# Column sums for the l2 norms of a four-mixer transformer block: one float32 product replaced by two float32r products on split squares

## The chip, the cores and the metric

The kernel runs on one core of a Trainium2 chip. The metric is the device time of one launch, in microseconds (us). The trace is one profiled execution on that core. The engines are named as the profile names them: PE is TensorE (PEld its weight loads), DVE is VectorE, ACT is ScalarE, POOL is GpSimd, SP is SyncE. SBUF is the on-chip memory, PSUM the banks into which TensorE writes.

## The reference, cut to what matters

Two layers (`DEPTH = 2`) over 512 tokens of width 1024. Each mixes four branches; the first is a gated delta rule, and its queries and keys (4 heads of 128 each) are normalised by head:

```
def l2norm(x, eps=1e-6):
    xf = x.astype(jnp.float32)
    return xf * lax.rsqrt(jnp.sum(xf * xf, axis=-1, keepdims=True) + eps)

qkv = jax.nn.silu(causal_dwconv(gdn_qkv, conv_w))
qa, ka, va = jnp.split(qkv, [GDN_HEADS * GDN_DK, 2 * GDN_HEADS * GDN_DK], axis=-1)
qa = l2norm(to_heads(qa, GDN_HEADS)) * GDN_DK ** -0.5
ka = l2norm(to_heads(ka, GDN_HEADS))
...
oa = gated_delta_chunked(qa, ka, va, beta, g)
```

## The kernel before

Activations lie with features on the 128 partitions and tokens along the free axis, so a head of queries or keys is one tile of 128 x 512: `aQ[:, 0:4]` and `aK[:, 0:4]`. A sum over a head is then a sum over partitions, and TensorE makes it as a product with a matrix of ones, which leaves the sum in every row of a PSUM bank.

All large products are made from split operands. A float32 number is split into a float32r part (`_hi`) and a float32r remainder (`_lo`), and a product is three passes: hi x hi, lo x hi, hi x lo. The weights come in units of 256 rows x 512 columns: SyncE loads them into `stage`, GpSimd rounds them (L581, `ring_hi`) and subtracts (L583, `ring_lo`) into a ring of four units, and TensorE consumes one unit in 24 matmuls of 512 columns (L1722, `unit`). GpSimd may fill a ring slot when TensorE has done with the unit four earlier.

Every engine has its own program order, written out by hand; semaphores tie them. TensorE runs the jobs `aq`, `ak`, `aab` and `av` (the raw queries, keys, gate columns and values) and puts small products between the units of `av`, in `value_unit`:

- after unit 0: `l2_sums(0, 1, 2, 3)`, the four query tiles (L1827)
- after unit 1: `gates_by_token` (L1833, writes tile `ab`), `l2_sums(4, 5, 6, 7)` for the keys, and the product `gc` (L1849)
- halfway through unit 2: `gt` (L1867), which first waits until VectorE has copied `gc` out (L1323)

ScalarE's order there: for the queries, Silu and then Square into `q_sq` (L727, L733); for the keys Silu; and, once the first query sum is there, four rounds of Square of key tile i (L733, into the same four slots of `q_sq`, so it waits for query sum i), Ln and Exp of query sum i (L738, L740). Then four small operations for the gates (L760 to L764), then Ln and Exp of the key sums.

VectorE's order there: the convolutions of the eight tiles (L1291, L1293), `qk_normed` of the four queries (L1299), the gate numbers (L1307 to L1319), `qk_normed` of the four keys, and the copy L1323.

The sums and the small tiles use the four PSUM banks `mix0` to `mix3` in turn. `gc` is in `mix1`, which key sum 4 held: TensorE can write it when `qk_normed(4)` has freed the bank.

Of the kernel before, what the change touches and what calls it, by code (L numbers as in the profile page):

```python
# [19 lines left out]
ALU = mybir.AluOpType  # L20
ACT = mybir.ActivationFunctionType
AX_X = mybir.AxisListType.X

P = 128
# [258 lines left out]
def mixer_keys():  # L283
# [50 lines left out]
    "a_LTm0": 10, "a_LTm1": 10, "a_S0": 3, "a_ab": 1, "a_arg": 16, "a_attd": 4, "a_dec": 4, "a_decc": 8, "a_ed": 4,  # L334
    "a_g": 2, "a_kbe": 4, "a_ln": 8, "a_lt": 4, "a_lt0": 4, "a_ltc": 4, "a_ltq": 4, "a_nrm": 4, "a_ohi": 4,
    "a_olo": 4, "a_one": 2, "a_out": 4, "a_qd": 4, "a_rhi": 2, "a_rs": 8, "a_sc": 3, "a_silu": 12, "a_small": 2,
    "a_smallact": 4, "a_sq": 8, "a_tap": 24, "a_z": 4, "a_zero": 1, "an_rs": 4, "an_sq": 4, "b_exp": 36, "b_fc": 3,
    "b_fexp": 3, "b_max": 12, "b_nm": 12, "b_ohi": 5, "b_olo": 5, "b_rhi": 9, "b_rlo": 9, "b_rp": 9, "b_share": 2,
    "b_sum": 3, "b_zinv": 1, "b_zln": 1, "big_done0": 43, "big_done1": 43, "big_done2": 38, "big_done3": 38,
    "big_free0": 43, "big_free1": 43, "big_free2": 38, "big_free3": 38, "c_act": 40, "c_add": 8, "c_bias": 3,  # L340
# [14 lines left out]
def hybrid_kernel(nc, ins, out):  # L355
    ctx = ExitStack()
    with ctx:
# [111 lines left out]
        def sem(name):  # L469
            if name not in sems:  # L470
                sems[name] = ctx.enter_context(nc.semaphore(name))
            return sems[name]
# [3 lines left out]
        def upto(name, count):  # L476

            return sem(name), count + layer[0] * PER_LAYER.get(name, 0)
# [45 lines left out]
        def f32(ap):  # L524
            return ap.bitcast(F32)
# [61 lines left out]
        def scalar_layer(act, l):  # L587
# [141 lines left out]
            def qk_squares(i):  # L729
                if i >= 4:  # L730
                    mix_wait(act, ("l2", i - 4))
                act.wait_ge(*upto("a_silu", i + 1))
                A(q_sq[:, i % 4, :], (aQ, aK)[i // 4][:, i % 4, :], ACT.Square).then_inc(sem("a_sq"), 1)  # L733

            def qk_root(i):

# [381 lines left out]
        def vector_layer(dve, l):  # L1118
# [176 lines left out]
            def qk_normed(i):  # L1295
                dve.wait_ge(*upto("a_rs", i + 1))
                b, _ = MIX["l2", i]
                t = (aQ, aK)[i // 4][:, i % 4, :]
                mix_free(STT(t, t, DK ** -0.5 if i < 4 else 1.0, mxb[b][:, :], ALU.mult, ALU.mult), ("l2", i))  # L1299

            for i in range(8):
                conv(i)
            for i in range(4):
                qk_normed(i)
            ps = mix_wait(dve, "ab")
            abv = ps[:, 0:32].rearrange("p (b c) -> p b c", b=4)
# [377 lines left out]
        def tensor_layer(pe, l):  # L1684
# [86 lines left out]
            def done(ins_, key):  # L1771
                ins_.then_inc(sem(home(key)[1]), 1)
# [50 lines left out]
            def l2_sums(*tiles):  # L1823
                for i in tiles:
                    ps = tile_of(("l2", i))
                    pe.wait_ge(*upto("a_sq", i + 1))
                    done(MM(ps[:, :], f32(ones_r[:, 0:1]).to_broadcast((P, P)), q_sq[:, i % 4, :], start=True, stop=True), ("l2", i))  # L1827

            def gates_by_token():
                ps = tile_of("ab")  # L1830
# [564 lines left out]
```

## Time and profile before

| | us |
|---|---|
| median of 3 runs | 2326.91 |
| lowest and highest | 2325.54, 2327.57 |
| span of the profiled execution, first to last instruction | 2324.0 |
| TensorE busy | 2297.4 (99% of the span) |
| GpSimd, VectorE, ScalarE busy | 1282.2, 851.0, 751.4 |
| mean granted TensorE clock | 0.997 |

The profiled execution has no other time of its own than its span; the median is 2.9 us above it, which is what lies before the first and after the last instruction and the difference between executions.

A row of the timeline gives start, duration, engine, line, operation, output<-inputs, shapes and count; in square brackets stand the idle time of the engine before it and what ended that. Rows of one engine can overlap: TensorE's matmuls are pipelined, so the distance between starts, and not a duration, says how long each one holds the engine. A VectorE or GpSimd operation that was ready but could not run yet has the waiting time inside its duration.

### The profile page before, as it was taken

What the parts mean: (1) busy time and instruction counts of PE and PEld (TensorE: products, weight loads), DVE (VectorE), ACT (ScalarE), POOL (GpSimd) and SP (SyncE); (2) the same over time, 40 slices, a digit from 0 to 9 for tenths busy, and PEclk for the clock granted to TensorE, in tenths of its full rate; (3) what the DMA queues carried; (4) which work ended last, traced back from release to release, by engine and by line L of the source; (5) the groups of instructions that cost most, each with busy time, mean ns of one, the idle gap of its engine ahead of it and who ended that gap; (6) DMA issues with size and microseconds to landing.
All of it is one profiled execution on the core that took longest, in us unless ns stands there. A gap on an engine that the chain in (4) does not pass through costs nothing.

```text
span 2324.0 us, 31844 instructions
## 1 busy us (share of the span) xinstructions
PE 2297.4 (99%) x13054; PEld 1870.2 (80%) x13054; DVE 851.0 (37%) x1350; ACT 751.4 (32%) x1505; POOL 1282.2 (55%) x732
## 2 busy tenths in 40 slices
PE   8999999999999999999999999999999999999998
PEld 7788877877877888888887888778778778888887
DVE  4543225334445521123355430254243445112233
ACT  5633226213035321122355341451230544112121
POOL 5513654554554566677655136546555445666874
PEclk9999999999999999999999999999999999999999
DMA  4311331322221243322222113213222213333331
GB/s 151 91 38 47 95 87 46 118 82 86 75 89 52 92 124 92 100 94 97 82 79 85 36 54 93 73 60 115 84 88 84 74 60 101 108 100 94 97 100 64
DMA packets 105904, 196.72 MB, mean 85 GB/s; under 512 B 8480, under 2 KB 18848, under 8 KB 105504
## 3 DMA queue, kind: packets, MB, share of 16 engines
q1 hardware_dynamic: 104608, 188.40, 26.8%
q10 hardware_dynamic: 1152, 6.29, 0.8%
q8 instruction: 104, 1.70, 0.3%
q14 instruction: 40, 0.33, 0.0%
HBM read 192.57 MB, written 2.10 MB: 84 GB/s over the span
## 4 chain that ended last, share of the span: by engine, by line
PE 96%; ACT 2%; DVE 2%; issue 1%; DMA 0%; DVEq 0%; ACTq 0%
PE big L1722 71%; PE mix L1722 9%; PE mix L1867 5%; PE big L2074 1%; PE mix L2042 1%; PE mix L2144 1%; PE mix L2053 1%; PE mix L1827 1%; PE mix L2272 0%; PE mix L2225 0%; PE mix L1781 0%; ACT o_hi L618 0%; PE mix L2209 0%; PE mix L2195 0%; PE mix L1999 0%
## 5 line engine op out<-in xcount | busy, mean ns | idle before, releaser
L583 POOL TENSOR_TENSOR ring_lo<-stage,ring_hi 128x1024 fp32r<-128x1024 f32 (+3 forms) x364 | 912.4, 2507 | 30.4
L581 POOL TENSOR_SCALAR ring_hi<-stage 128x1024 fp32r<-128x1024 f32 (+3 forms) x364 | 371.3, 1020 | 987.9 <-PE big L1722 906.6
L1722 PE MATMUL big<-h_hi,ring_hi 128*128 128x512 f32 (+1 forms) x1888 | 720.6, 382 | 3.0 <-DVE h_lo L1173 1.8
L1722 PE MATMUL big<-h_hi,ring_lo 128*128 128x512 f32 (+1 forms) x1888 | 709.3, 376 | 0.0
L1722 PE MATMUL big<-h_lo,ring_hi 128*128 128x512 f32 (+1 forms) x1888 | 709.2, 376 | 0.0
L1722 PEld LDWEIGHTS big<-h_hi,ring_hi 128*128 128x128 f32 x1888 | 355.4, 188 | 75.1 <-issue 8.6
L1722 PEld LDWEIGHTS big<-h_lo,ring_hi 128*128 128x128 f32 x1888 | 355.4, 188 | 65.7
L1722 PEld LDWEIGHTS big<-h_hi,ring_lo 128*128 128x128 f32 x1888 | 355.7, 188 | 62.9 <-issue 1.4
L1663 DVE TENSOR_TENSOR h_lo<-scr,h_hi 128x1024 fp32r<-128x1024 f32 x64 | 84.7, 1323 | 248.5 <-ACT h_hi L1091 248.5
L1722 PE MATMUL big<-ring_hi,h_hi 128*128 128x512 f32 x448 | 174.2, 390 | 0.0
L1722 PE MATMUL big<-ring_lo,h_hi 128*128 128x512 f32 x448 | 174.1, 390 | 0.0
L1722 PE MATMUL big<-ring_hi,h_lo 128*128 128x512 f32 x448 | 173.7, 389 | 0.0
L1091 ACT ACTIVATE h_hi<-scr 128x1024 fp32r<-128x1024 f32 x64 | 68.5, 1070 | 262.2 <-PE big L1722 260.2
L1674 DVE SCALAR_TENSOR_TENSOR scr<-big,scr 128x512 f32<-128x512 f32 x64 | 44.3, 692 | 254.5 <-ACT scr L1100 254.3
L1722 PE MATMUL mix<-ring_hi,h_hi 128*128 128x512 f32 x320 | 125.0, 391 | 0.0
L1722 PE MATMUL mix<-ring_hi,h_lo 128*128 128x512 f32 x320 | 124.6, 389 | 0.0
L1722 PE MATMUL mix<-ring_lo,h_hi 128*128 128x512 f32 x320 | 124.5, 389 | 0.0
L1100 ACT ACTIVATE scr<-big 128x512 f32<-128x512 f32 x64 | 38.3, 598 | 262.1 <-PE big L1722 261.3
L1722 PEld LDWEIGHTS big<-ring_hi,h_hi 128*128 128x128 f32 x448 | 84.1, 188 | 18.4 <-issue 0.7
L1722 PEld LDWEIGHTS big<-ring_hi,h_lo 128*128 128x128 f32 x448 | 84.1, 188 | 17.7
L1722 PEld LDWEIGHTS big<-ring_lo,h_hi 128*128 128x128 f32 x448 | 83.8, 188 | 18.0 <-POOL ring_lo L583 1.0
L1722 PE MATMUL big<-o_hi,ring_hi 128*128 128x512 f32 x224 | 90.2, 403 | 1.0 <-ACT scr L676 0.9
(304 smaller groups left out, 2758.0 us busy)
## 6 DMA issues: line engine op xcount, KB each, us to landing
stage<-in_w_in SPq DMA_DIRECT2D x168, 512.0 KB, 3.5
stage<-in_w_mlp_in SPq DMA_DIRECT2D x64, 512.0 KB, 3.7
stage<-in_w_mlp_out SPq DMA_DIRECT2D x64, 512.0 KB, 3.6
stage<-in_w_o SPq DMA_DIRECT2D x16, 512.0 KB, 3.6
stage<-in_w_br_a SPq DMA_DIRECT2D x8, 512.0 KB, 3.6
stage<-in_w_br_c SPq DMA_DIRECT2D x8, 512.0 KB, 3.6
stage<-in_w_br_d SPq DMA_DIRECT2D x8, 512.0 KB, 3.6
stage<-in_w_br_b SPq DMA_DIRECT2D x8, 512.0 KB, 3.6
```

What stands on the lines that cost most here:

```text
L581: nc.gpsimd.tensor_scalar(rH[jw][0:pp, r, 0:kk, 0:job.n], w, 1.0, 0.0, ALU.mult, ALU.add).then_inc(sem("w_hi"), 1)
L583: nc.gpsimd.tensor_tensor(rL[jw][0:pp, r, 0:kk, 0:job.n], w, f32(rH[jw][0:pp, r, 0:kk, 0:job.n]), ALU.subtract).then_inc(sem("w_ready"), 1)
L1091: A(hH[:, q:q + 2, :], fT[:, 2 * u:2 * u + 2, :], ACT.Copy).then_inc(sem("f_hi"), 1)
L1100: A(fT[:, 4 * g + i, :], ps[:, :], ACT.Relu).then_inc(sem("f_relu"), 1)
L1663: TT(hL[:, q:q + 2, :], fT[:, 2 * u:2 * u + 2, :], f32(hH[:, q:q + 2, :]), ALU.subtract).then_inc(sem("f_lo"), 1)
L1674: big_free(STT(fT[:, k, :], ps[:, :], 0.0, fT[:, k, :], ALU.max, ALU.mult), (f"up{g}", i))
L1722: ins_ = MM(o_, a_, r_, start=s0, stop=s1)
L1827: done(MM(ps[:, :], f32(ones_r[:, 0:1]).to_broadcast((P, P)), q_sq[:, i % 4, :], start=True, stop=True), ("l2", i))
L1867: return MM(o_, a_, b_, start=True, stop=True)
L2042: i = MM(c_bank[u][:, at:at + w], hv(cK, h)[:, j * P:(j + 1) * P], hv(cQ, h)[:, j * P:], start=opens, stop=True, skip_group_check=True)
L2053: MM(c_bank[u][:, :], rot_r[:, 2 * P:3 * P], part[:, u, :], start=False, stop=True, skip_group_check=True)
L2074: r = MM(c_out[e * DH:e * DH + DH, j * P:], cV[:, j, (2 * p + e) * DH:(2 * p + e + 1) * DH], c_A[:, u, at:at + S - j * P], start=j == 0, s ...
```

## The change

The squares are now split, and the sum is two float32r passes in place of one float32 product, for all eight tiles of each layer. The head means later in the layer (L2017) keep their float32 product.

- Queries, ScalarE: Square twice, into `q_sq` (float32) and into `oH` (float32r, the rounded square).
- Keys, ScalarE: Square once, into `oH`. VectorE squares the keys into `q_sq` with a multiply of the tile by itself.
- VectorE: `square_lo(i)` subtracts, `oL = q_sq - oH`, for all eight tiles.
- TensorE: ones x `oH`, then ones x `oL`, into the same bank; it now waits for `square_lo(i)` where it waited for the Square.

`oH` and `oL` are existing tensors, free at this point of the layer.

```diff
 def qk_squares(i):
     if i >= 4:
         mix_wait(act, ("l2", i - 4))
     act.wait_ge(*upto("a_silu", i + 1))
-    A(q_sq[:, i % 4, :], (aQ, aK)[i // 4][:, i % 4, :], ACT.Square).then_inc(sem("a_sq"), 1)
+    x = (aQ, aK)[i // 4][:, i % 4, :]
+    if i < 4:
+        A(q_sq[:, i, :], x, ACT.Square)
+    A(oH[:, i % 4, :], x, ACT.Square).then_inc(sem("a_sq"), 1)
...
-            for i in range(8):
+            def square_lo(i):
+                dve.wait_ge(*upto("a_sq", i + 1))
+                if i >= 4:
+                    dve.wait_ge(*upto("a_sqk", i - 3))
+                TT(oL[:, i % 4, :], q_sq[:, i % 4, :], f32(oH[:, i % 4, :]), ALU.subtract).then_inc(sem("a_sqlo"), 1)
+
+            for i in range(4):
                 conv(i)
+            for i in range(4):
+                square_lo(i)
+            for i in range(4, 8):
+                conv(i)
+            for i in range(4):
+                dve.wait_ge(*upto("a_silu", i + 5))
+                dve.wait_ge(*upto("a_sqlo", i + 1))
+                TT(q_sq[:, i, :], aK[:, i, :], aK[:, i, :], ALU.mult).then_inc(sem("a_sqk"), 1)
             for i in range(4):
+                square_lo(i + 4)
                 qk_normed(i)
...
-                    pe.wait_ge(*upto("a_sq", i + 1))
-                    done(MM(ps[:, :], f32(ones_r[:, 0:1]).to_broadcast((P, P)), q_sq[:, i % 4, :], start=True, stop=True), ("l2", i))
+                    pe.wait_ge(*upto("a_sqlo", i + 1))
+                    ones = ones_r[:, 0:1].to_broadcast((P, P))
+                    MM(ps[:, :], ones, oH[:, i % 4, :], start=True, stop=False)
+                    done(MM(ps[:, :], ones, oL[:, i % 4, :], start=False, stop=True), ("l2", i))
```

VectorE's order from the last convolution to the first gate number, before (L1293 is the end of a convolution, L1299 `qk_normed`, L1307 the first gate number):

```order
L1293 SCALAR_TENSOR_TENSOR scr<-mix3,lw,scr 128x509
L1299 SCALAR_TENSOR_TENSOR scr<-scr,mix0 128x512
L1299 SCALAR_TENSOR_TENSOR scr<-scr,mix1 128x512
L1299 SCALAR_TENSOR_TENSOR scr<-scr,mix2 128x512
L1299 SCALAR_TENSOR_TENSOR scr<-scr,mix3 128x512
L1307 TENSOR_TENSOR st<-mix0,lw 128x16
```

The same stretch of the changed kernel (its lines are numbered anew: L1319 squares the keys, L1308 is `square_lo`, L1302 `qk_normed`, L1325 the first gate number):

```order
L1296 SCALAR_TENSOR_TENSOR scr<-mix3,lw,scr 128x509
L1319 TENSOR_TENSOR scr<-scr 128x512 x4
L1308 TENSOR_TENSOR o_lo<-scr,o_hi 128x512
L1302 SCALAR_TENSOR_TENSOR scr<-scr,mix0 128x512
L1308 TENSOR_TENSOR o_lo<-scr,o_hi 128x512
L1302 SCALAR_TENSOR_TENSOR scr<-scr,mix1 128x512
L1308 TENSOR_TENSOR o_lo<-scr,o_hi 128x512
L1302 SCALAR_TENSOR_TENSOR scr<-scr,mix2 128x512
L1308 TENSOR_TENSOR o_lo<-scr,o_hi 128x512
L1302 SCALAR_TENSOR_TENSOR scr<-scr,mix3 128x512
L1325 TENSOR_TENSOR st<-mix0,lw 128x16
```

Eight operations with both inputs in SBUF now stand ahead of the first gate number.

TensorE's order at the second group, from the gates (L1833) to `gc` (L1849), before:

```order
L1833 MATMUL mix0<-consts,scr 128x8 x4
L1827 MATMUL mix1<-scr,ones_r 128x512
L1827 MATMUL mix2<-scr,ones_r 128x512
L1827 MATMUL mix3<-scr,ones_r 128x512
L1827 MATMUL mix0<-scr,ones_r 128x512
L1849 MATMUL mix1<-st,consts 128x16
```

The same place in the changed kernel (L1853 the gates, L1846 and L1847 the two passes, L1869 `gc`):

```order
L1853 MATMUL mix0<-consts,scr 128x8 x4
L1846 MATMUL mix1<-o_hi,ones_r 128x512
L1847 MATMUL mix1<-o_lo,ones_r 128x512
L1846 MATMUL mix2<-o_hi,ones_r 128x512
L1847 MATMUL mix2<-o_lo,ones_r 128x512
L1846 MATMUL mix3<-o_hi,ones_r 128x512
L1847 MATMUL mix3<-o_lo,ones_r 128x512
L1846 MATMUL mix0<-o_hi,ones_r 128x512
L1847 MATMUL mix0<-o_lo,ones_r 128x512
L1869 MATMUL mix1<-st,consts 128x16
```

Each tile has two instructions there instead of one; the one of before is two records in the trace. The banks and the place of every other instruction are the same.

## Rows read from the trace of the kernel before

**Rows 1.** Page, part 1: engine, busy us (share of the span), instructions.
```profile
PE 2297.4 (99%) x13054; PEld 1870.2 (80%) x13054; DVE 851.0 (37%) x1350; ACT 751.4 (32%) x1505; POOL 1282.2 (55%) x732
```

**Rows 2.** Timeline, TensorE, layer 0: start us, us, engine, line, op, tiles.
```profile
73.66 3.59 PE L1827 MATMUL mix<-scr,ones_r 128*128 128x512 f32 x8
...
77.32 0.39 PE L1722 MATMUL big<-h_hi,ring_lo 128*128 128x512 f32 x1
...
82.66 0.41 PE L1833 MATMUL mix<-consts,scr 8*128 8x8 f32 x4
...
83.00 3.70 PE L1827 MATMUL mix<-scr,ones_r 128*128 128x512 f32 x8
...
86.53 0.29 PE L1849 MATMUL mix<-st,consts 128*128 128x16 f32 x2
...
89.63 0.40 PE L1867 MATMUL mix<-consts,st 128*16 128x128 f32 x4
```

**Rows 3.** Timeline, TensorE, start of an existing float32r pair and of its successor.
```profile
523.62 0.40 PE L2010 MATMUL mix<-o_hi,ones_r 128*128 128x512 f32 x1
...
523.86 0.40 PE L2011 MATMUL mix<-o_lo,ones_r 128*128 128x512 f32 x1
...
524.09 2.32 PE L2144 MATMUL mix<-scr 128*128 128x512 f32 x8
```

**Rows 4.** Timeline, ScalarE and VectorE, layer 0, around both norm groups.
```profile
74.71 0.63 ACT L733 ACTIVATE scr<-scr 128x512 f32<-128x512 f32 x1 [2.66 <-PE mix L1827]
...
76.35 0.62 ACT L733 ACTIVATE scr<-scr 128x512 f32<-128x512 f32 x1
...
81.38 0.69 DVE L1299 SCALAR_TENSOR_TENSOR scr<-scr,mix 128x512 f32<-128x512 f32 x1 [0.95 <-ACT mix L740]
...
83.10 0.17 DVE L1307 TENSOR_TENSOR st<-mix,lw 128x16 f32<-128x16 f32 x1 [1.04 <-PE mix L1833]
...
85.41 0.69 DVE L1299 SCALAR_TENSOR_TENSOR scr<-scr,mix 128x512 f32<-128x512 f32 x1 [0.55 <-ACT mix L740]
...
89.32 0.17 DVE L1323 COPY st<-mix 128x16 f32<-128x16 f32 x1
```

**Rows 5.** Timeline, GpSimd and VectorE, layer 0, around the last four convolutions.
```profile
59.87 1.53 DVE L1291 SCALAR_TENSOR_TENSOR scr<-mix,lw,scr 128x511 f32<-128x511 f32 x2 [10.82 <-ACT scr L722]
...
67.98 1.05 POOL L581 TENSOR_SCALAR ring_hi<-stage 128x1024 fp32r<-128x1024 f32 x1
...
68.11 0.75 DVE L1293 SCALAR_TENSOR_TENSOR scr<-mix,lw,scr 128x509 f32<-128x509 f32 x1
...
69.11 2.40 POOL L583 TENSOR_TENSOR ring_lo<-stage,ring_hi 128x1024 fp32r<-128x1024 f32 x1
...
79.56 2.41 POOL L583 TENSOR_TENSOR ring_lo<-stage,ring_hi 128x1024 fp32r<-128x1024 f32 x1
```

**Rows 6.** Timeline, GpSimd and VectorE, where both read SBUF at once.
```profile
457.39 1.06 POOL L581 TENSOR_SCALAR ring_hi<-stage 128x1024 fp32r<-128x1024 f32 x1 [2.21 <-PE big L1722]
...
457.96 1.02 DVE L1505 TENSOR_TENSOR o_lo<-scr,o_hi 128x512 fp32r<-128x512 f32 x1 [21.56 <-ACT o_hi L839]
...
458.53 2.71 POOL L583 TENSOR_TENSOR ring_lo<-stage,ring_hi 128x1024 fp32r<-128x1024 f32 x1
...
458.91 2.88 DVE L1513 TENSOR_TENSOR scr<-scr 128x512 f32<-128x512 f32 x1
...
467.42 0.69 DVE L1513 TENSOR_TENSOR scr<-scr 128x512 f32<-128x512 f32 x1
```

**Rows 7.** Timeline, TensorE, layer 0: the stretch ahead of a fallen clock.
```profile
733.31 4.89 PE L2272 MATMUL mix<-scr,consts 3*128 3x512 f32 x14
```

**Rows 8.** Windows: length, busy (x) PE, PEld, DVE, ACT, POOL; PEclk, DMA share, GB/s.
```profile
733.30:738.40 5.10, 5.10 (x16) 1.69 (x16) 3.60 (x6) 2.49 (x4) 0.00 (x0) 1.00 0.03 10
738.40:741.90 3.50, 3.50 (x10) 2.74 (x10) 3.50 (x5) 2.69 (x4) 3.02 (x2) 0.55 0.02 5
```

**Rows 9.** Timeline, GpSimd, the same place in layer 1.
```profile
1219.85 1.05 POOL L581 TENSOR_SCALAR ring_hi<-stage 128x1024 fp32r<-128x1024 f32 x1
```

More of the change, by code:

```diff
@@ L336 @@
     "a_olo": 4, "a_one": 2, "a_out": 4, "a_qd": 4, "a_rhi": 2, "a_rs": 8, "a_sc": 3, "a_silu": 12, "a_small": 2,
-    "a_smallact": 4, "a_sq": 8, "a_tap": 24, "a_z": 4, "a_zero": 1, "an_rs": 4, "an_sq": 4, "b_exp": 36, "b_fc": 3,
+    "a_smallact": 4, "a_sq": 8, "a_sqk": 4, "a_sqlo": 8, "a_tap": 24, "a_z": 4, "a_zero": 1, "an_rs": 4, "an_sq": 4, "b_exp": 36, "b_fc": 3,
     "b_fexp": 3, "b_max": 12, "b_nm": 12, "b_ohi": 5, "b_olo": 5, "b_rhi": 9, "b_rlo": 9, "b_rp": 9, "b_share": 2,
```

## The prediction, made before the change was run

> **What bounds the kernel now.** I read the page's busy times first: TensorE is busy for 99% of the span and GpSimd, next to it, for 55% [rows 1]. So a microsecond less on TensorE is a microsecond less of time, if no wait takes its place; and whatever VectorE or ScalarE get more of costs nothing, unless TensorE waits for it. The rest is read from the timeline around the eight sums. I give times of layer 0; layer 1 has the same pattern 1151.87 us later: the L581 of GpSimd that starts at 67.98 in the one is at 1219.85 in the other [rows 5, 9]. What holds for one layer is counted twice.
>
> Three things are to be seen. First, TensorE's price: eight records from 73.66, and the second matmul of the next unit at 77.32 [rows 2]. With its predecessor 0.23 ahead of it (half of the 0.47 us of the pair in rows 3), the four tiles took 77.09 - 73.66 = 3.43 us, 0.86 each. Second, TensorE is not alone: ScalarE's first key Square waits for the first query sum (74.71), its rounds are 1.64 us long (74.71 to 76.35), `qk_normed(3)` follows at 81.38, and only then VectorE can take up the gates; at 83.10 it was released by TensorE's gate product, after 1.04 us of idling [rows 4]. Third, the chain behind L1307 has no slack on its far end: `qk_normed(4)` at 85.41, the copy of `gc` at 89.32 ends at 89.49, and TensorE, which has to have it, goes on at 89.63 [rows 2, 4]. TensorE got there 0.1 us after it was ready. From L1307 on everything is a chain through ScalarE's Ln and Exp, so **TensorE passes L1867 earlier only by as much as L1307 starts earlier**, and later by as much as it starts later.
>
> **What the change removes on TensorE.** Two float32r passes with ones as weights take 524.09 - 523.62 = 0.47 us [rows 3]. Per tile 0.86 - 0.47 = 0.39 us less; 1.56 per group of four, 3.1 per layer, 6.2 for 16 tiles. The second group's gates would be reached at 82.66 - 1.56 = 81.10 and its sums at 81.44 instead of 83.00.
>
> **What it adds on ScalarE.** Four more Squares of 0.63 us each on the queries [rows 4]. They run before the keys' convolutions, in the same idle stretch as the queries' subtractions (below), and I cost them at nothing. Were that cover gone, it would be 2.5 us per layer. For the keys it is one Square for one. The first sum is there sooner (0.24 + 0.40 us after 73.66 instead of 0.43 + 0.59), so ScalarE's rounds start 0.4 us sooner: `qk_normed(3)` could run at 81.0 and end at 81.7. The queries' `square_lo` stand between two groups of convolutions, where VectorE idles 10.82 us [rows 5]; also nothing.
>
> **What it adds on VectorE, where it counts.** Four squares and four subtractions with both inputs in SBUF. Alone such an operation takes 0.69 us (the last of [rows 6]). But beside GpSimd it does not run alone. L1505 was issued at 457.96, in the middle of GpSimd's L581 (457.39 to 458.45), and ended at 458.98, 0.53 after it. GpSimd's L583, issued at 458.53, then took 2.71 us instead of 2.40 and ended at 461.24, 2.26 after L1505. And L1513, already issued at 458.91, took 2.88 us and ended 0.55 after L583. So the two engines take turns: **each such VectorE operation waits for the GpSimd operation in progress, and a waiting GpSimd operation goes ahead of the next one of VectorE** [rows 6]. `qk_normed` and the convolutions read one input from PSUM and kept their 0.69 to 0.75 us beside GpSimd [rows 4, 5].
>
> From 67.98 GpSimd works without a pause until 79.56 + 2.41 = 81.97 [rows 5]: L581, then L583, three times L581 and L583, that is seven operations after the first. VectorE's eight operations start at 68.8, when the last convolution is over. Taking turns, with 0.55 us for one of VectorE, 2.25 for L583 and 0.92 for L581 (like L583, 0.13 less than alone, as it is issued by then), the ends are: square 0 69.58, L583 71.83, square 1 72.38, L581 73.30, square 2 73.85, L583 76.10, square 3 76.65, L581 77.57, `square_lo(4)` 78.12, L583 80.37, `square_lo(5)` 80.92, L581 81.84, `square_lo(6)` 82.39, L583 84.64, `square_lo(7)` 85.19. The four `qk_normed` fit between. The last of them follows at 85.1 and L1307 at **85.72 instead of 83.10: 2.6 us later**, where it could have been at 81.6. The copy ends at 92.1 and TensorE goes on at 92.17 instead of 89.63: 2.5 us later per layer, 5.1 us in all. All that TensorE saves is lost in waiting: about 2.4 us for `square_lo(7)` and 3.0 us for `qk_normed(4)` (85.41 + 0.69 + 2.6 = 88.7), which holds the bank of `gc`. GpSimd, being ahead by units, doesn't stop TensorE: the unit after the sums is split at 76.1 and wanted at 88.9.
>
> In the four squares both inputs are the same tile, and no row shows such an operation beside GpSimd. If they didn't wait, the turns would begin with `square_lo(4)` at 75.0: L581 and L583 to 76.5 and 79.0, `square_lo(5)` 79.5, L581 80.4, `square_lo(6)` 81.0, L583 83.2, `square_lo(7)` 83.8, L1307 84.3: 1.2 us later than now. That is the lower end, 2.4 us in all. I take the upper one, since the operation is like its neighbours in all but the address. The Trainium skill ("SBUF — State Buffer", section "Who interferes with whom") counts inputs in SBUF, not tiles: two of them contend with a GpSimd instruction that reads SBUF, one doesn't; the rule's side is the 5.1 us, and no run here shows it yet.
>
> **The clock.** TensorE will be nearly idle from 82.9 to 88.8, but for one pair of 0.47 us. In the trace, 4.89 us of matmuls with 3 rows [rows 7] were followed by 3.5 us at a granted clock of 0.55, mostly at 1.2 GHz in place of 2.4 [rows 8]; TensorE lost 3.5 x 0.45 = 1.6 us. I expect the clock to fall here too, in the idle stretch or behind it. What of it passes while TensorE waits costs nothing, and L1867 has 0.25 us of slack (88.8 + 3.1 = 91.9 against 92.17). Between 0 and 1.6 us per layer I take 1.0, so 2.0 in all.
>
> **Sum.** 5.1 + 2.0 = 7.1 us on a span of 2324.0, and so on the median: 2326.9 + 7.1 = **2334.0**. The profiled span is 2.9 us below the median of the runs; I take that to stay.
>
> **The rivals**, each for both layers, added to 2326.9.
> - *The turns as above, the clock doesn't fall*: +5.1, 2332.0. For it: the trace shows no case of a pure wait of 3 us with a full clock before it.
> - *The squares don't take turns*: 2329.3. TensorE's waits are then short, and the clock stays.
> - *No turns in this stretch at all* (not slower): L1307 at 81.6, 1.5 us earlier, behind `qk_normed(3)`; 3.0 us gained, 2323.9. It decides if VectorE's subtractions run beside GpSimd in 0.69 us. Against it stand rows 6.
> - *All of TensorE's saving arrives*: 6.2 us, 2320.7. It needs a chain that moves 3.1 us per layer, but ScalarE's rounds move 0.4; against it is the zero slack at the copy [rows 2, 4].
> - *GpSimd wins between L583 and the next L581 too*, which it issues with no gap: VectorE then waits for two operations at each turn, GpSimd is through at 83.3, and the four `square_lo` and `qk_normed` follow back to back, 1.2 us a pair: L1307 at 88.0, 4.9 us later; +9.8 and the clock's 2.0, 2338.7. Rows 6 show only the handover from L581 to L583.
>
> **How the numbers follow.** Forecast 0.50; clock stays 0.20; squares free 0.08; no turns 0.10; all saved 0.05; double turns 0.07. The range from 2329.0 to 2339.5 takes in the first three and the last, 0.85. 0.2% is 4.7 us, about what a measurement can tell from no change: slower is above 2331.6. That is the forecast, the double turns, and half of the clock case, whose 2332.0 lies on the edge: 0.67. Faster is the case with all saved, 0.05. The rest, 0.28, is within.
>
> **What would show it.** Right: in the profile after, VectorE's four squares (L1319) and the last four `square_lo` (L1308) with durations of 1.5 to 2.9 us instead of 0.69; GpSimd's L583 at 2.7; TensorE waiting for `square_lo(7)` over 2 us and before `gc` (L1869) about 3 us, twice; a granted clock of 0.5 for some microseconds after 86. Wrong: durations of 0.69 there, or L1325 starting less than 84.3. If the fall of the clock lasts over two stretches like that of rows 8, the time goes to the range's upper half.

## The result and the profile after

The changed kernel takes 2338.76 us (median of 9 runs, 2335.48 to 2344.91), the kernel before 2326.91 (9 runs beside them, 2324.68 to 2337.09). The ratio is 1.005, with a 95% interval of 1.0037 to 1.0063: slower, by 11.9 us of the medians. The profiled execution has a span of 2334.8 against 2324.0, 10.8 more. The forecast was 7.1 more for both. The direction and the chain over VectorE came as said; the term for the clock was too small.

Page of the changed kernel, part 1, the answer to [rows 1]:

```profile
PE 2299.9 (99%) x13054; PEld 1874.2 (80%) x13054; DVE 884.7 (38%) x1374; ACT 755.7 (32%) x1513; POOL 1288.1 (55%) x732
```

TensorE's busy time rose by 2.5 us although it was given 6.2 us less to do: matmuls at a lower clock count as busy for longer. VectorE has 24 instructions and 34 us more, twice the 24 x 0.69 = 16.6 us that they would need alone: the other half is waiting inside operations.

**VectorE and GpSimd**, timeline of the changed kernel, layer 0. (All of it stands 0.32 us later than in the trace before, since the last convolution already does: 68.43 against 68.11 in [rows 5]. TensorE is 0.3 us later by 20 us, ahead of everything that the change touches.)

```profile
69.10 7.89 DVE L1319 TENSOR_TENSOR scr<-scr 128x512 f32<-128x512 f32 x4
76.91 1.53 DVE L1308 TENSOR_TENSOR o_lo<-scr,o_hi 128x512 fp32r<-128x512 f32 x1
...
78.97 2.30 DVE L1308 TENSOR_TENSOR o_lo<-scr,o_hi 128x512 fp32r<-128x512 f32 x1
...
81.78 0.92 DVE L1308 TENSOR_TENSOR o_lo<-scr,o_hi 128x512 fp32r<-128x512 f32 x1
...
83.23 2.24 DVE L1308 TENSOR_TENSOR o_lo<-scr,o_hi 128x512 fp32r<-128x512 f32 x1
85.39 0.68 DVE L1302 SCALAR_TENSOR_TENSOR scr<-scr,mix 128x512 f32<-128x512 f32 x1
85.99 0.16 DVE L1325 TENSOR_TENSOR st<-mix,lw 128x16 f32<-128x16 f32 x1
```
```profile
69.45 2.71 POOL L583 TENSOR_TENSOR ring_lo<-stage,ring_hi 128x1024 fp32r<-128x1024 f32 x1
72.14 1.49 POOL L581 TENSOR_SCALAR ring_hi<-stage 128x1024 fp32r<-128x1024 f32 x1
...
76.41 1.50 POOL L581 TENSOR_SCALAR ring_hi<-stage 128x1024 fp32r<-128x1024 f32 x1
77.99 2.72 POOL L583 TENSOR_TENSOR ring_lo<-stage,ring_hi 128x1024 fp32r<-128x1024 f32 x1
```

These are the turns of the prediction, and the four key squares take part in them, though both inputs are the same tile: 7.89 us for four operations that need 0.69 each alone. `square_lo(5)`, issued at 78.97 behind L583 (77.99), ends at 81.27, 0.56 after L583's end at 80.71. The `square_lo` at 81.78 is short, 0.92 us, because it was issued late into GpSimd's L581 (80.69 to 82.17); its end was forecast at 82.39 + 0.32 = 82.71 and is 82.70. L1325 was forecast at 85.72 + 0.32 = 86.04 and started at 85.99.

**TensorE**, timeline of the changed kernel at the second group; to be read beside [rows 2]:

```profile
81.40 0.41 PE L1853 MATMUL mix<-consts,scr 8*128 8x8 f32 x4
...
83.36 0.50 PE L1846 MATMUL mix<-o_hi,ones_r 128*128 128x512 f32 x1 [0.72 <-DVE scr L1302]
...
86.12 0.50 PE L1846 MATMUL mix<-o_hi,ones_r 128*128 128x512 f32 x1 [2.03 <-DVE scr L1302]
...
89.11 0.58 PE L1869 MATMUL mix<-st,consts 128*128 128x16 f32 x2 [1.79 <-DVE scr L1302]
...
90.53 0.63 PE L1740 MATMUL big<-h_lo,ring_hi 128*128 128x512 f32 x1
90.96 0.63 PE L1740 MATMUL big<-h_hi,ring_hi 128*128 128x512 f32 x1
...
94.63 0.40 PE L1887 MATMUL mix<-consts,st 128*16 128x128 f32 x4
```

Three waits stand here, 4.5 us together; before there was none of them. Behind the last, the matmuls of the next unit are 0.43 us apart instead of 0.23. VectorE had copied `gc` out by 92.37 (its L1341: 92.20 and 0.17), but TensorE reached `gt` (L1887) only at 94.63.

**The granted clock** of the stretch, windows of the changed kernel (length, busy (x) of PE, PEld, DVE, ACT, POOL; granted clock, DMA share, GB/s), and then the same two windows of the kernel before:

```profile
84.00:86.60 2.60, 0.57 (x3) 0.43 (x3) 2.49 (x6) 0.00 (x0) 0.92 (x1) 1.00 0.21 35
86.60:93.40 6.80, 5.01 (x15) 3.78 (x14) 3.38 (x9) 4.80 (x12) 2.85 (x2) 0.56 0.17 64
```
```profile
84.00:86.60 2.60, 2.60 (x9) 1.16 (x7) 1.32 (x6) 2.54 (x8) 0.00 (x0) 1.00 0.36 138
86.60:93.40 6.80, 6.80 (x36) 5.29 (x35) 3.74 (x10) 2.17 (x5) 3.43 (x2) 1.00 0.21 57
```

And of the changed kernel, layer 1's sums and the stretch that answers to [rows 8]:

```profile
1244.80:1251.60 6.80, 5.79 (x16) 4.11 (x15) 3.44 (x10) 4.80 (x12) 2.79 (x2) 0.52 0.20 68
```
```profile
742.50:749.50 7.00, 7.00 (x16) 4.63 (x15) 6.45 (x6) 5.84 (x6) 3.74 (x2) 0.52 0.02 4
```

Behind TensorE's waits the clock is near 1.2 GHz for some 7 us, in both layers. The fall behind L2272 (L2292 here), which [rows 8] show for 3.5 us, lasts 7.0 us in this trace.

**Where the 10.8 us of the span are.** A useful measure is the time from the gate products (L1853, before L1833) to `gt` (L1887, before L1867). It was 6.97 us in layer 0 [rows 2] and is 13.23 now; in layer 1 it was 6.94 (1234.51 to 1241.45) and is 12.69 (1239.67 to 1252.36). With the 1.56 us saved at the first group that is 4.7 and 4.2 us per layer. In each 2.5 are the later first gate number. The rest, 2.2 and 1.7, is the clock. The longer fall at 742 adds 1.6: from the first matmul of L2292 to the next product into a `mix` bank from `oH` it is 20.69 us (738.39 to 759.08), where it was 19.11 (733.31 to 752.42). With the 0.3 from ahead of the sums that is 4.7 + 4.2 + 1.6 + 0.3 = 10.8.

The 1.6 us are not shown to be the change's doing. The length of that fall differs without it. In the trace of the kernel before, the same place in layer 1 (its L2272 starts at 1885.29) has the longer fall, and in a kernel of the experiments that has no split squares and no wait in the stage ("the two moves alone", below) so has layer 0. Windows, first of the kernel before, then of that kernel:

```profile
1890.00:1896.00 6.00, 6.00 (x14) 3.87 (x13) 3.79 (x5) 4.65 (x6) 3.82 (x2) 0.51 0.00 0
```
```profile
738.00:744.00 6.00, 6.00 (x14) 4.46 (x14) 5.71 (x5) 4.96 (x5) 3.73 (x2) 0.50 0.01 3
```

### The profile page after: what moved, and what is told of

Read it like the earlier page. It is cut to its first block, busy times and chain, and to the rows that moved or that the text cites. A ratio compares the mean times of both kernels' runs of the same rounds, so it can differ in the third digit from the quotient of the medians.

```text
span 2334.8 us, 31892 instructions
## 1 busy us (share of the span) xinstructions
PE 2299.9 (99%) x13054; PEld 1874.2 (80%) x13054; DVE 884.7 (38%) x1374; ACT 755.7 (32%) x1513; POOL 1288.1 (55%) x732
## 4 chain that ended last, share of the span: by engine, by line
PE 94%; DVE 3%; ACT 2%; issue 1%; DMA 0%; DVEq 0%; ACTq 0%
PE big L1740 70%; PE mix L1740 9%; PE mix L1887 5%; PE big L2094 1%; PE mix L2062 1%; PE mix L2164 1%; PE mix L2073 1%; PE mix L2292 0%; PE mix L2245 0%; DVE o_lo L1308 0%; PE mix L1799 0%; ACT o_hi L618 0%; PE mix L2229 0%; PE mix L2215 0%; PE mix L2019 0%
## 5 line engine op out<-in xcount | busy, mean ns | idle before, releaser
L583 POOL TENSOR_TENSOR ring_lo<-stage,ring_hi 128x1024 fp32r<-128x1024 f32 (+3 forms) x364 | 915.2, 2514 | 30.4
L581 POOL TENSOR_SCALAR ring_hi<-stage 128x1024 fp32r<-128x1024 f32 (+3 forms) x364 | 374.4, 1028 | 992.8 <-PE big L1740 911.3
```

Source lines behind the costliest of these rows:

```text
L581: nc.gpsimd.tensor_scalar(rH[jw][0:pp, r, 0:kk, 0:job.n], w, 1.0, 0.0, ALU.mult, ALU.add).then_inc(sem("w_hi"), 1)
L583: nc.gpsimd.tensor_tensor(rL[jw][0:pp, r, 0:kk, 0:job.n], w, f32(rH[jw][0:pp, r, 0:kk, 0:job.n]), ALU.subtract).then_inc(sem("w_ready"), 1)
```

## The experiments

Each ran beside the kernel before, on the same chip, in three sittings on different chips. The kernel before took 2327.00 us in the first (passes alone, first hold, squares on ScalarE, filler), 2326.49 in the second (squares alone, second hold, fastest kernel, moves alone) and 2326.12 in the third (float32 back, moves without the hold, ScalarE with the moves). Ratios are to it. "The stage" below is the time from the gate products to `gt`, 6.97 us before and 13.23 in the changed kernel (layer 0).

### The passes alone

```diff
-                A(q_sq[:, i % 4, :], (aQ, aK)[i // 4][:, i % 4, :], ACT.Square).then_inc(sem("a_sq"), 1)
+                A(oH[:, i % 4, :], (aQ, aK)[i // 4][:, i % 4, :], ACT.Square).then_inc(sem("a_sq"), 1)
...
-                    done(MM(ps[:, :], f32(ones_r[:, 0:1]).to_broadcast((P, P)), q_sq[:, i % 4, :], start=True, stop=True), ("l2", i))
+                    ones = ones_r[:, 0:1].to_broadcast((P, P))
+                    MM(ps[:, :], ones, oH[:, i % 4, :], start=True, stop=False)
+                    done(MM(ps[:, :], ones, oH[:, i % 4, :], start=False, stop=True), ("l2", i))
```

> The kernel before, with only TensorE's part of the change: ScalarE writes the rounded square into oH, and both float32r passes read oH (the remainder oL is left out, so its part of the sum is missing and the high part counts twice). VectorE and GpSimd do exactly what they did before. It measures what the two passes are worth when nothing else moves. Theory (the chain behind the first gate number has no slack): TensorE's 8 tiles per layer take 0.47 us instead of 0.86, 3.1 us less per layer, but only as much arrives as the first gate number (L1307) moves: from 83.10 to about 81.7, so about 1.5 us per layer, 3.0 in all, 2324 us; a wait ahead of gc grows by the other 1.6 us. Rival (all of TensorE's saving arrives): 6.2 us less, 2320.7. Second rival (the clock falls in the new wait): nothing or less than 1 us arrives.

Measured: 2324.41 us, ratio 0.9986 (0.9976 to 0.9996), 2.6 us less than the kernel before. Timeline of this kernel, TensorE and VectorE:

```profile
81.07 0.41 PE L1835 MATMUL mix<-consts,scr 8*128 8x8 f32 x4
...
84.73 0.37 PE L1851 MATMUL mix<-st,consts 128*128 128x16 f32 x2 [1.23 <-DVE scr L1299]
...
88.03 0.40 PE L1869 MATMUL mix<-consts,st 128*16 128x128 f32 x4
```
```profile
81.61 0.17 DVE L1307 TENSOR_TENSOR st<-mix,lw 128x16 f32<-128x16 f32 x1
```

L1307 moved from 83.10 to 81.61, and L1869 from 89.63 to 88.03: of 3.1 us that TensorE saves per layer, 1.6 arrive. Of the rest, 1.23 stand as a wait ahead of `gc` and about 0.1 ahead of `gt`. So the zero slack at the copy was read rightly, and the change without its side effects was worth half of what TensorE saves. The rival with 6.2 us less is out.

### The squares alone

```diff
+            for i in range(4):
+                dve.wait_ge(*upto("a_silu", i + 5))
+                TT(oL[:, i, :], aK[:, i, :], aK[:, i, :], ALU.mult)
             for i in range(4):
                 qk_normed(i)
```

> The kernel before, plus the four key squares on VectorE alone, behind the last convolution; their results go to a tensor that nobody reads there. Both inputs of each are the same tile. It isolates whether such squares take turns with GpSimd, and what they cost when they have slack behind them: qk_normed(0) is bound by ScalarE's rounds. Theory (turns, but idle time hides them): the four squares take about 7.9 us together, as in the changed kernel (69.10 to 76.99), GpSimd's L583 2.7 instead of 2.4; they end at about 76.8, within 0.4 us of where qk_normed(0) stood (76.5), and qk_normed(3) and L1307 stay at 81.4 and 83.1. So the time is that of the kernel before, 2327 plus or minus 1.5 us. Rival (the squares themselves are the 11.6 us): L1307 moves by over 1 us and the time rises by 3 or more.

Measured: 2327.58 us, ratio 1.0005 (0.9995 to 1.0015). VectorE's timeline in this kernel:

```profile
68.67 7.81 DVE L1305 TENSOR_TENSOR o_lo<-scr 128x512 fp32r<-128x512 f32 x4
76.40 0.67 DVE L1299 SCALAR_TENSOR_TENSOR scr<-scr,mix 128x512 f32<-128x512 f32 x1
...
82.98 0.17 DVE L1310 TENSOR_TENSOR st<-mix,lw 128x16 f32<-128x16 f32 x1 [1.04 <-PE mix L1836]
```

The squares alone take the same turns, 7.81 us, and cost nothing that can be measured: VectorE was idle there, and L1310 starts where L1307 did. The turns are harmful only where something waits behind them.

### GpSimd held, at the wrong place and at the right one

Two kernels, with one line's difference. The first holds GpSimd ahead of the third unit of the values until `square_lo(7)` is made:

```diff
+                if (job.name, i) == ("av", 2):
+                    pool.wait_ge(*upto("a_sqlo", 8))
```

> The changed kernel, but GpSimd doesn't split the unit wanted behind the sums' place (the third of the values) until VectorE has made the last square_lo. VectorE keeps its eight added operations and their order; only their company is gone. Theory (the two engines take turns at SBUF): the four key squares take about 0.6 us each instead of 1.5 to 2.7, the four square_lo 0.69, qk_normed(3) is bound by ScalarE's rounds again, and L1325 starts at about 82.0 instead of 85.99. The gates' chain starts some 1.4 us earlier than in the kernel before, TensorE has no idle stretch of over 2 us there, its clock stays full behind the sums: about 3 us less than the kernel before, 2324 us, and 14 to 15 less than the changed kernel. Rival (eight more operations in VectorE's own order are the cost, whatever GpSimd does): L1325 stays later than 84, the durations are 0.69 but VectorE is simply late, and the time stays above 2333. Second rival (GpSimd, held back, becomes the bound): TensorE waits for ring_lo of that unit or of one behind it by 1 us or more, and the time doesn't fall below the kernel before.

Measured: 2335.60 us (2329.24 to 2348.09), ratio 1.0031 (1.0012 to 1.005). The 2324 us expected were missed by 12, and the interval overlaps the changed kernel's, so no gain is shown. The squares and subtractions did what it said (four squares in 4.82 us, L1327 at 81.40), and then came this, in the timelines of this kernel:

```profile
81.85 2.36 DVE L1332 TENSOR_SCALAR st<-st 128x16 f32<-128x16 f32 x1
```
```profile
81.76 2.42 POOL L585 TENSOR_TENSOR ring_lo<-stage,ring_hi 128x1024 fp32r<-128x1024 f32 x1
```
```profile
86.73 0.58 PE L1871 MATMUL mix<-st,consts 128*128 128x16 f32 x2 [3.43 <-DVE scr L1304]
```

GpSimd, let go at 80.6, was in L585 when VectorE came to the gate numbers. An operation on 16 columns, 0.17 us long otherwise, waited 2.2 us for it, in the middle of the chain to `gc`. TensorE waited 3.43 us and the clock was at 0.52 from 86.0 to 92.8. The company had not been removed but moved.

The second holds GpSimd ahead of the fourth unit, until the gate numbers are ready:

```diff
+                if (job.name, i) == ("av", 3):
+                    pool.wait_ge(*upto("a_g", 2))
```

> The changed kernel, but GpSimd doesn't split the fourth unit of the values (not the third, as in the run that held GpSimd before) until the gate numbers of VectorE are ready, so that neither the four square_lo of the keys nor the small gate operations meet it. The third unit is split beside the key squares, which have slack; the fourth is wanted by TensorE only behind 90. In the earlier run the hold ended between square_lo(7) and the gate numbers, and GpSimd's L585 (81.76 to 84.18) then held the small operation L1332 (81.85 to 84.21). Theory (what counts is the VectorE chain from qk_normed(3) to the gates, and the wait ahead of gc, which brings the clock down): the last three square_lo take 0.69 us, L1327 starts at about 81.5, the small operations 0.17 each, gc at 84.8 behind a wait of about 1.3 us, a granted clock of 1.0 from 84 to 96. The time is that of the passes alone: 2324 to 2325, 2 to 3 us less than the kernel before, 14 less than the changed one. Rival (in each kernel with both the passes and VectorE's work the clock falls behind the sums): 2330 or more. Rival (GpSimd late): TensorE waits for ring_lo behind 90.

Measured: 2326.99 us (2320.93 to 2332.41), ratio 0.9998 (0.9987 to 1.0008): 12 us less than the changed kernel, with the same arithmetic and the same instructions but for one wait. Timelines of this kernel, VectorE and TensorE:

```profile
80.27 0.68 DVE L1310 TENSOR_TENSOR o_lo<-scr,o_hi 128x512 fp32r<-128x512 f32 x1
...
81.71 0.17 DVE L1327 TENSOR_TENSOR st<-mix,lw 128x16 f32<-128x16 f32 x1
```
```profile
84.84 0.37 PE L1871 MATMUL mix<-st,consts 128*128 128x16 f32 x2 [1.23 <-DVE scr L1304]
```

The stage is 6.97 us in both layers, as with the passes alone, and TensorE waits for no `ring_lo`. The four key squares still took turns here (7.88 us together), with slack behind them; only the `square_lo` and the gate operations were freed. So the turns of the `square_lo` are the cause of the later first gate number; the added operations as such are not. But the time is not the 2324 to 2325 of the theory. In this trace (and in that of the passes alone) the clock is down at another place, where it was up before. Windows of this kernel, then of the kernel before:

```profile
118.00:130.40 12.40, 12.40 (x140) 10.37 (x137) 3.55 (x9) 1.95 (x7) 3.40 (x2) 0.50 0.16 45
```
```profile
118.00:130.40 12.40, 12.36 (x302) 10.94 (x299) 7.58 (x19) 3.34 (x12) 3.40 (x2) 1.00 0.22 72
```

That is a stretch of products with 64 rows and 32 columns, 35 us behind the sums. The fall costs 5.9 us: between the same two groups of these products lie 24.21 us in this trace (114.47 to 138.68) and 18.35 in the kernel before (115.96 to 134.31). The profiled run is the slowest of the 11 of this kernel (2332.41), so the median holds less of it. What decides whether the clock falls there is open (below).

### The squares on ScalarE

```diff
+            for i in range(4):
+                act.wait_ge(*upto("a_silu", i + 5))
+                act.wait_ge(*upto("a_sqlo", i + 1))
+                A(q_sq[:, i, :], aK[:, i, :], ACT.Square).then_inc(sem("a_sqk"), 1)
...
-            for i in range(4):
-                dve.wait_ge(*upto("a_silu", i + 5))
-                dve.wait_ge(*upto("a_sqlo", i + 1))
-                TT(q_sq[:, i, :], aK[:, i, :], aK[:, i, :], ALU.mult).then_inc(sem("a_sqk"), 1)
```

> The changed kernel, but ScalarE makes the float32 squares of the keys too, in its idle time ahead of the first query sum; VectorE's order keeps the four square_lo of the keys and loses the four squares. GpSimd is untouched. Theory (turns, and all eight operations take part in them): half of the turns are gone. The turns begin with square_lo(4) at 75.0 and L1325 starts at about 84.6, where it was 85.99; about 1.2 us per layer later than the kernel before, little of the clock's fall: 2329 us, some 9 to 10 less than the changed kernel. If the turns cost nothing and the delay is in the number of operations, each operation counts 0.69: four fewer give 2.8 us per layer at most, and only if VectorE is never idle there. If L1325 starts at 83.4 or earlier, the phase of the two engines decides more than the number of operations.

Measured: 2333.51 us (2327.78 to 2342.09), ratio 1.0028 (1.0013 to 1.0044). The 2329 us expected were missed by 4.5. L1325 was at 82.05, not at 84.6: the phase did it. ScalarE's rounds pace the `square_lo`, and the first two of the four were issued within 0.02 us of GpSimd's next operation, ran at once, and it was GpSimd that waited. The second of them, on both engines' timelines:

```profile
76.58 0.68 DVE L1312 TENSOR_TENSOR o_lo<-scr,o_hi 128x512 fp32r<-128x512 f32 x1
```
```profile
76.57 2.95 POOL L583 TENSOR_TENSOR ring_lo<-stage,ring_hi 128x1024 fp32r<-128x1024 f32 x1
```

But again a small gate operation met GpSimd, and TensorE waited (VectorE's and TensorE's timelines of this kernel):

```profile
82.39 1.42 DVE L1329 SCALAR_TENSOR_TENSOR st<-st 128x16 f32<-128x16 f32 x1
```
```profile
86.41 0.45 PE L1869 MATMUL mix<-st,consts 128*128 128x16 f32 x2 [3.00 <-DVE scr L1306]
...
91.14 0.40 PE L1887 MATMUL mix<-consts,st 128*16 128x128 f32 x4
```

From 86.40 to 89.80 the granted clock was 0.52. This trace has falls behind it in both layers too (0.59 from 118.0 to 134.5 and 0.57 from 1331 to 1347), and it is the slowest of the kernel's 12 runs, with a span of 2340.3.

### Filler for the clock

```diff
+                    for _ in range(12 if i == 5 else 0):
+                        MM(ps[:, :], ones, hH[:, 0, :], start=True, stop=True)
                     MM(ps[:, :], ones, oH[:, i % 4, :], start=True, stop=False)
```

> The changed kernel plus twelve float32r products in TensorE's order, ones by a tile of activations, into the bank of key sum 5 just ahead of its own two passes (which overwrite them). They are 12 x 0.24 = 2.8 us of matmuls that serve nothing, in the stretch in which TensorE waited 0.72 + 2.03 + 1.79 us. Theory (the fallen clock behind this wait costs about 2 us per layer and more later): the chain over VectorE is not touched, L1325 stays at about 86.0 and the copy L1341 at about 92.2, but the matmuls behind it run at a granted clock of 1.0 and L1887 starts at about 92.5 instead of 94.63. 4 us less than the changed kernel in all, 2334 to 2335, although TensorE does 5.6 us more work. Rival (the clock's fall has another cause, or costs nothing): the same time as the changed kernel or more, since L1887 then hangs on what it hung on, and the filler can only delay.

Measured: 2336.17 us, ratio 1.0043 (1.0026 to 1.006); 2.6 us less than the changed kernel by the medians, with 5.6 us more work on TensorE. The two intervals overlap, so the medians (5 runs here) don't show a gain by themselves; the stage does. Timeline of TensorE and the windows of this kernel:

```profile
83.21 3.05 PE L1847 MATMUL mix<-h_hi,ones_r 128*128 128x512 f32 x12 [0.72 <-DVE scr L1302]
...
89.00 0.37 PE L1871 MATMUL mix<-st,consts 128*128 128x16 f32 x2 [1.34 <-DVE scr L1302]
...
92.30 0.40 PE L1889 MATMUL mix<-consts,st 128*16 128x128 f32 x4
```
```profile
86.60:93.40 6.80, 5.36 (x26) 3.73 (x25) 3.95 (x11) 4.71 (x12) 3.44 (x2) 1.00 0.16 61
```

L1325 stayed at 85.87, and `gt` came at 92.30 instead of 94.63, right behind the copy (92.08 and 0.17). The stage is 11.02 and 11.00 us instead of 13.23 and 12.69. So the fallen clock behind the waits is worth 2.2 and 1.7 us, 3.9 in all, where the prediction had 2.0; and it falls because TensorE waits, since work without any use keeps it up. The 4 us don't show in this trace's span (2334.3 against 2334.8): it has falls at 738 to 750 (0.54 and 0.61 in windows of 6 us) and at 1344 (0.72) that the changed kernel's trace has less of.

### The rest of the saving

The kernel of the second hold, with `gc` moved behind six matmuls of the next unit, and its copy moved two `qk_normed` forward:

```diff
+                if i == "gc":
                     pe.wait_ge(*upto("a_g", 2))
...
-            unit(JOB["av"], 2, (0, 1))
+            unit(JOB["av"], 2, (0,))
+            value_unit("gc")
+            unit(JOB["av"], 2, (1,))
             value_unit(2)
...
-            for i in range(4, 8):
-                qk_normed(i)
+            qk_normed(4)
+            qk_normed(5)
             ps = mix_wait(dve, "gc")
             mix_free(V.tensor_copy(s_gc, ps[:, 0:16].rearrange("p (b h) -> p b h", b=4)), "gc")
+            qk_normed(6)
+            qk_normed(7)
```

> The kernel of the run with GpSimd held at the fourth unit, and two moves more: TensorE makes six matmuls of the next unit ahead of gc, and VectorE copies gc out behind qk_normed(5) instead of qk_normed(7). Theory (what is left of TensorE's saving is lost in the wait ahead of gc and in the copy): both waits go to 0, gt's transposes start at about 86.3 instead of 89.63, 3.3 us less per layer, of which the chain to g_rows behind qk_normed(7) may take back 0.3 to 1: 2320 to 2322, 5 to 6 us less than the kernel before. Rival (the work behind gt has no slack in the other engines' order either): the waits come back at the next products of L1889 and no more than 3 us arrive. Rival (the clock falls more often once TensorE has less of the dense matmuls there): 2325 or more.

Measured: 2320.61 us, 2320.28 to 2321.66 in 9 runs, ratio 0.9969 (0.9958 to 0.9979). That is 5.9 us less than the kernel before (2326.49 beside it), with an interval wholly below 1, and 18 less than the changed kernel. TensorE's timeline in this kernel:

```profile
80.04 0.41 PE L1857 MATMUL mix<-consts,scr 8*128 8x8 f32 x4
...
83.72 0.35 PE L1874 MATMUL mix<-st,consts 128*128 128x16 f32 x2
85.49 0.40 PE L1892 MATMUL mix<-consts,st 128*16 128x128 f32 x4
```

No wait stands in the stage; it is 5.45 us, 1.52 less than before, and with the first group's 1.56 that is 3.1 us per layer, 6.2 in all, TensorE's whole saving. (The span is 5.6 us shorter: this trace is also 1.0 ahead by 20 us, since its clock was 1.00 from 12 to 18 and the kernel before had 0.76, and it loses 1.6 to a longer fall, from 729.18 to 749.88 in place of 733.31 to 752.42.) Three kernels say what of this is due to what. First, the two moves alone (the diff above without the hold) in the kernel before:

> The kernel before with only the two moves (six matmuls of the next unit ahead of gc; the copy of gc behind qk_normed(5)), no split squares and nothing held. It is the measure beside which the run with both is to be read. Theory: TensorE didn't wait ahead of gc in the kernel before, and 0.1 us ahead of gt, so 0.1 to 0.3 us per layer: 2326.5, no change that can be measured. Rival (the copy's place had cost TensorE more than the trace shows): 3 us or more less, and the gain of the run with both would be this one.

Measured: 2329.26 us (2326.09 to 2342.81), ratio 1.0012 (0.9999 to 1.0026), and a stage of 6.97 us, as before: no gain from the moves without the passes. Second, the fastest kernel with a float32 product back in place of the two passes:

```diff
-                    ones = ones_r[:, 0:1].to_broadcast((P, P))
-                    MM(ps[:, :], ones, oH[:, i % 4, :], start=True, stop=False)
-                    done(MM(ps[:, :], ones, oL[:, i % 4, :], start=False, stop=True), ("l2", i))
+                    done(MM(ps[:, :], f32(ones_r[:, 0:1]).to_broadcast((P, P)), f32(oH[:, i % 4, :]), start=True, stop=True), ("l2", i))
```

> The fastest kernel (GpSimd held at the fourth unit, gc and its copy later) with TensorE's part of the change undone: each sum is one float32 product of ones with the rounded square again, so the remainder is left out of the sums, while ScalarE and VectorE do all they did. Theory (with the waits gone, TensorE's work there is worth its full length): 16 tiles of 0.86 instead of 0.47 us, 6.2 us more than the fastest kernel: 2326.8, the time of the kernel before. Rival (part of the gain of that kernel came from the hold or from the moves): less than 5 us more.

Measured: 2328.98 us (2326.00 to 2342.70), ratio 1.001 (0.9996 to 1.0025), 8.4 more than the fastest kernel by the medians and 5.7 by the spans (2324.1 and 2318.4), with a stage of 6.96 again. Third, the fastest kernel without the hold on GpSimd (the two lines on `a_g` taken out):

> The changed kernel with the two moves of the fastest run (six matmuls ahead of gc; gc copied out behind qk_normed(5)), but GpSimd is not held. It takes the hold alone away from the fastest kernel. Theory (the hold, that is the turns, is most of it): square_lo(7) ends at about 85.4 as in the changed kernel, TensorE still waits 0.7 and 2.0 us for the banks of key sums 5 and 7, but no longer ahead of gc; gt at about 90.6, 0.7 later per layer than the kernel before, 1.3 us in all if the clock stays up, 5 if it falls behind the wait of 2.0: 2328 to 2332, 8 to 12 more than the kernel with the hold. Rival (the hold does nothing, the moves alone mend it): 2321 to 2323.

Measured: 2337.37 us, ratio 1.0047 (1.0031 to 1.0064), above my range of 2328 to 2332 for want of a larger clock term. Its timeline of TensorE has the waits of the changed kernel, except the one ahead of `gc`:

```profile
85.90 0.50 PE L1848 MATMUL mix<-o_hi,ones_r 128*128 128x512 f32 x1 [2.04 <-DVE scr L1302]
...
91.58 0.40 PE L1890 MATMUL mix<-consts,st 128*16 128x128 f32 x4
```

From 86.20 to 89.60 the granted clock was 0.54: it fell behind the waits of 0.71 and 2.04 us, though the one ahead of `gc` was gone. (I had named the banks of key sums 5 and 7; the waits are those of 5 and 6.) So with the moves around it the hold, which ends the turns of the `square_lo`, is worth 17 us by the medians and 12 by the spans (2330.4 and 2318.4). The moves without it gain nothing that can be measured: the interval overlaps the changed kernel's. Without a hold, but with the squares on ScalarE and the two moves:

> The kernel with the float32 squares of the keys on ScalarE, with the same two moves; GpSimd is not held. In the run without the moves L1325 started at 82.05, one of the small gate operations, L1329, waited 1.42 us for GpSimd, and TensorE waited 3.0 us ahead of gc, behind which the clock fell. Theory: gc now stands 1.4 us of matmuls later, the wait ahead of it is 1.6 instead of 3.0, gt at about 87.8 instead of 89.63, 1.8 us less per layer, and with a wait this short the clock stays at 1.00 (it stayed behind waits of 1.23): 2323 to 2324. Rival (a wait of 1.6 is enough to bring it down): 2326 to 2329. If it is at 2321, half of the turns cost nothing at all.

Measured: 2324.54 us (2321.41 to 2328.22), ratio 0.9992 (0.9984 to 1.0), at most just faster than the kernel before. Layer 0 came as expected, on TensorE's timeline of this kernel:

```profile
86.53 0.37 PE L1872 MATMUL mix<-st,consts 128*128 128x16 f32 x2 [1.63 <-DVE scr L1306]
...
88.30 0.40 PE L1890 MATMUL mix<-consts,st 128*16 128x128 f32 x4
```

In layer 1, with the same wait of 1.63 us, the clock was 0.86 from 1236 to 1242 and 0.85 from 1242 to 1248, so it stayed up behind the wait in one layer and fell in the other.

## Why the prediction came out as it did

- **TensorE's saving** of 0.39 us a tile: right. The passes are 0.23 us apart, the gates came at 81.40 - 0.32 = 81.08 (forecast 81.10), and the fastest kernel shows all 6.2 us.
- **ScalarE's squares free**: right. The rounds started 0.4 us sooner (74.64 - 0.32 against 74.71), and the kernel of the second hold shows L1327 at 81.71 with all of them in place, 0.1 from the passes alone (81.61), which lack them.
- **The turns on VectorE**: right to 0.05 us at the first gate number (85.99 against 86.04), and so were the 2.5 us per layer and the durations, but for one: the sign of being right asked for 1.5 to 2.9 us in all of the last four `square_lo`, and one took 0.92, as the forecast's own chain of ends gives it. The choice for the squares of one and the same tile, for which no row stood, was settled by the squares alone: 7.81 us for four. The rule of the Trainium skill ("SBUF — State Buffer", section "Who interferes with whom"), that inputs in SBUF count, holds here too.
- **TensorE's waits**: their sum was forecast as 5.4 us, of which 4.5 came; the place was named wrongly. It doesn't wait for `square_lo(7)`, whose result is there at 85.47. It waits for the banks of key sums 5 and 6, which `qk_normed(2)` and `qk_normed(3)` free; these stand behind `square_lo` in VectorE's order. The end of the chain was the same, so the 5.1 us don't hang on it.
- **The clock**: this is the term that was mis-sized. It was to cost "between 0 and 1.6 us per layer", of which I took 1.0, and 2.0 in all. Behind TensorE's waits it cost 2.2 and 1.7, as the filler shows, 3.9 together, and both lie above the bound. The bound came from the fall of 3.5 us in layer 0 [rows 8]. The same place in layer 1 of the same trace has one nearly twice as long (0.51 from 1890 to 1896), which the bound leaves out. That a fall could last over two such stretches I named as what would push the time up; it should have been the bound.
- **What the sum left out**: 1.6 us for the longer fall at 742, which is not shown to come from the change, and 0.3 from ahead of the sums, which doesn't. With the clock as measured the span's sum is 5.1 + 3.9 + 1.6 + 0.3 = 10.9, for 10.8. The median grew by 1.1 more than the span: the profiled run now lies 4.0 us below the median, and I took 2.9 to stay.
- **Rivals**: no turns, and free squares, fell by the trace itself; all of the saving arriving fell by the passes alone; double turns fell by GpSimd's rows, where each L581 waited 0.45 us for VectorE too. That this last rival's 2338.7 is the measured median to 0.1 us is chance: its L1307 at 88.0 didn't come.

Open: why the clock is down from 118 to 130 in the traces of three kernels whose waits ahead of `gc` are 1.23 to 3.0 us, and not in those of the fastest one, of the kernel before, or of the changed kernel itself. No run here changes that stretch alone. Open too is how far the change makes the fall at 742 longer: one trace of each kernel can't tell.

## What to carry to other kernels

Before work is given to VectorE, look at what GpSimd does at that time: an operation with both inputs in SBUF costs there what GpSimd's operation in progress still has to run, however small it is itself, and this is free only as long as nobody waits behind it. To hold GpSimd back was the better cure here: 2326.99 us against 2333.51 with half of VectorE's work moved to ScalarE, and 2320.61 against 2324.54 with the two moves on top. But the hold must end behind the whole chain, small operations included. And a wait that opens on TensorE may have to be charged twice, once for itself and once for the matmuls at half speed behind it: in the stage the clock fell behind every longest wait of 2.0 us or more, in one layer of two behind 1.63, and not behind 1.23 or 1.34. Once the turns are gone, what is left of such a wait goes by putting some of the next unit's matmuls ahead of the waiting product; while they stood, that gained nothing.

## What the runs showed of the hardware

- A VectorE operation of 128 x 16 was held by GpSimd like a large one: 2.36 us instead of 0.17 for L1332 (max with a constant, one input in SBUF), 1.42 for L1329 (two inputs in SBUF). The first is not covered by a count of inputs. The Trainium skill ("SBUF — State Buffer", section "Who interferes with whom") names `tensor_scalar` among the operations that can enter a mode in which VectorE contends with GpSimd; the 2.36 us agree, though no run here tells the mode.
- Who goes first can't be read from the starts in the trace when they are 0.01 us apart: with the squares on ScalarE, `square_lo` (76.58) ran at once in 0.68 us, although GpSimd's L583 is shown 0.01 us ahead of it (76.57), and it was L583 that took 2.95 us. With the two moves it was the same (76.66 and 76.65, 0.68 and 2.96 us).
- The granted clock goes with the spread between runs of one kernel. In the first sitting the kernel before took 2324.6 to 2328.1 us in runs with a mean clock of 0.996 or 0.997, and 2334 to 2335 with 0.993; the hold at the wrong place gave 2329 with 0.996 and 2348 with 0.987. The fastest kernel had 0.997 in all of its 9 runs. A change of 0.3% has to be read from the stage's length in the trace as well as from the median.
